# A one-core two-block transformer kernel: both memory attentions reordered by pairs of heads, cross-attention roots on GpSimd

## The reference

```python
def memory_attention(h, mem_n, wq, wk, wv, wo):          # 4 heads of 256
    q = (h @ wq).reshape(B, S, MEM_HEADS, MEM_HEAD_DIM)
    k, v = ...                                           # from mem_n
    s = jnp.einsum('bshd,bmhd->bhsm', q, k).astype(F32) * (MEM_HEAD_DIM ** -0.5)
    p = jax.nn.softmax(s, axis=-1).astype(v.dtype)
    return jnp.einsum('bhsm,bmhd->bshd', p, v).reshape(B, S, D) @ wo

def memory_cross_attention(h, mem_n, wq, wkv, q_g, k_g, wo):   # 4 heads of 128
    q = rms_norm_2((h @ wq).reshape(b, s, XA_HEADS, XA_HEAD_DIM), q_g)
    k, v = ...                                           # from mem_n, k normed
    logits = jnp.einsum("bshd,bmhd->bhsm", q.astype(jnp.float32), k.astype(jnp.float32)) * (XA_HEAD_DIM ** -0.5)
    p = jax.nn.softmax(logits, axis=-1)
    o = jnp.einsum("bhsm,bmhd->bshd", p, v.astype(jnp.float32)).astype(h.dtype)
    return o.reshape(b, s, XA_WIDTH) @ wo
```

## Time and profile before

| | us |
|---|---|
| three runs | 971.75, 972.66, 981.94 (median 972.66) |
| profiled execution, its own time | 978.42 |
| its span | 976.4 |
| TensorE busy in it | 910.1 (93%) |
| VectorE, ScalarE, GpSimd busy | 574.4, 406.6, 131.2 |
| mean granted TensorE clock | 0.958 |

### The profile page before, as it was taken

How to read it: one execution, slowest core, us unless ns; L and a number is a source line. 1 busy time by engine, 2 the same in 40 slices (tenths; PEclk the granted TensorE clock), 3 DMA queues, 4 the chain that set the end, 5 groups by cost and what they waited for, 6 DMA issues and landing times.

```text
span 976.4 us, 13578 instructions
## 1 busy us (share of the span) xinstructions
PE 910.1 (93%) x5642; PEld 789.4 (81%) x5642; DVE 574.4 (59%) x830; ACT 406.6 (42%) x554; POOL 131.2 (13%) x174
## 2 busy tenths in 40 slices
PE   6988998998999999999899888999998889999998
PEld 5986985686778999999687886677577679999997
DVE  4349456345359867775668983743454648555552
ACT  4348242334336445443546444312233426444440
POOL 0150000100010000000169860340000000000000
PEclk9997998999999999999998999799999799999999
DMA  8971444052236655654145231100163228656531
GB/s 289 288 231 48 179 166 147 27 195 92 80 136 231 209 186 171 210 174 130 44 134 171 88 130 44 44 1 4 40 215 114 60 76 290 195 181 202 178 130 44
DMA packets 92344, 136.01 MB, mean 139 GB/s; under 512 B 4435, under 2 KB 76763, under 8 KB 92028
## 3 DMA queue, kind: packets, MB, share of 16 engines
q1 hardware_dynamic: 90428, 129.90, 40.5%
q0 software_dynamic: 736, 2.63, 0.9%
q10 hardware_dynamic: 1120, 2.62, 0.8%
HBM read 133.56 MB, written 1.06 MB: 138 GB/s over the span
## 4 chain that ended last, share of the span: by engine, by line
PE 79%; DVE 11%; ACT 3%; issue 2%; POOL 2%; DMA 2%; SPq 0%; POOLq 0%; DVEq 0%; ACTq 0%
PE work L1973 30%; PE acc L1973 25%; PE work L1954 7%; PE work L2430 3%; DVE hT L1320 2%; DVE split_operands L1335 1%; PE acc L2464 1%; ACT act_junk L883 1%; PE work L2358 1%; PE work L2367 1%; DVE arena L1613 1%; PE work L1960 1%; DVE split_extra_slot L1335 1%; PE work L2125 1%; PE work L2227 1%
## 5 line engine op out<-in xcount | busy, mean ns | idle before, releaser
L1335 DVE TENSOR_TENSOR split_operands<-weight_ring,split_operands 128x2048 fp32r<-128x2048 f32 x72 | 165.8, 2305 | 89.6 <-ACT split_operands L903 89.1
L1973 PE MATMUL work<-split_operands 128*128 128x256 f32 x1680 | 208.1, 284 | 3.9 <-DVE split_operands L1335 3.9
L1973 PEld LDWEIGHTS work<-split_operands 128*128 128x128 f32 x1680 | 205.7, 193 | 6.2 <-issue 4.9
L1973 PE MATMUL acc<-split_operands 128*128 128x512 f32 x888 | 207.5, 390 | 1.8 <-DVE split_operands L1557 1.8
L1973 PEld LDWEIGHTS acc<-split_operands 128*128 128x128 f32 x888 | 165.1, 188 | 35.5 <-DVE split_operands L1557 2.0
L903 ACT ACTIVATE split_operands<-weight_ring 128x2048 fp32r<-128x2048 f32 x72 | 137.3, 1909 | 107.0 <-PE acc L1973 49.3
L1973 PE MATMUL work<-split_operands,split_extra_slot 128*128 128x256 f32 x1152 | 145.5, 287 | 4.5 <-DVE split_extra_slot L1335 4.5
L1973 PEld LDWEIGHTS work<-split_operands,split_extra_slot 128*128 128x128 f32 x1152 | 142.8, 195 | 6.7 <-issue 5.8
L890 ACT ACTIVATE arena<-work 128x512 f32<-128x512 f32 (+1 forms) x70 | 39.0, 560 | 167.6 <-PE work L1973 82.6
L1335 DVE TENSOR_TENSOR split_extra_slot<-weight_ring,split_extra_slot 128x2048 fp32r<-128x2048 f32 x34 | 78.4, 2307 | 41.1 <-ACT split_extra_slot L903 40.8
L903 ACT ACTIVATE split_extra_slot<-weight_ring 128x2048 fp32r<-128x2048 f32 x34 | 64.9, 1909 | 47.7 <-PE work L1973 17.8
(11 more groups left out here) (295 smaller groups left out, 953.2 us busy)
## 6 DMA issues: line engine op xcount, KB each, us to landing
weight_ring<-in_mlp_w SPq DMA_DIRECT2D x32, 1024.0 KB, 5.5
weight_ring<-in_w_up SPq DMA_DIRECT2D x22, 1024.0 KB, 5.1
weight_ring<-in_w_in SPq DMA_DIRECT2D x20, 1024.0 KB, 5.9
weight_ring<-in_w_down SPq DMA_DIRECT2D x11, 1024.0 KB, 5.0
weight_ring<-in_w_out SPq DMA_DIRECT2D x8, 1024.0 KB, 4.9
weight_ring<-in_w_mk SPq DMA_DIRECT2D x4, 1024.0 KB, 5.9
weight_ring<-in_w_mv SPq DMA_DIRECT2D x4, 1024.0 KB, 6.1
weight_ring<-in_w_mq SPq DMA_DIRECT2D x4, 1024.0 KB, 5.4
```

Source lines behind the costliest of these rows:

```text
L1335: dve.tensor_tensor(slot[:, 1, :], weights(split_units[i], 2048), slot[:, 0, :], ALU.subtract).then_inc(low_ready, 1)
L1973: ins = pe.matmul(out, lhs(p), rhs(q), start=(start and n == 0), stop=(stop and n == 2))
```

## The change

Four heads are two pairs. Scores, softmax, transposes and values are now done pair by pair. In the first attention the scores of pair 0 come after three of four query products, and the fourth product stands between them and their transposes; the first unit of `wo` stands between the transposes of pair 1 and the values of pair 1. In the cross attention the second query product is cut in halves (one head each), the sums and scores of pair 0 stand between the halves; `xwo`'s first unit is issued in pieces, with the last tile of transposes and the values of pair 1 between them. The one-column sums go to `acc` banks, by pair. Sqrt and reciprocal become an add on VectorE and a power on GpSimd (`xq_roots`), and ScalarE does one small exponential earlier, so that its table is loaded there. ScalarE's and VectorE's programs are reordered to match, weight splits included.

```diff
     norm("mem")
-    tiles.extend(("mq", c) for c in range(4))
-    tiles.extend(("ms", t, hp) for t in range(TT) for hp in range(2))
-    tiles.extend(("mpT", t, hp) for t in range(TT) for hp in range(2))
-    tiles.extend(("mo", c) for c in range(4))
+    tiles.extend(("mq", c) for c in range(3))
+    tiles.extend(("ms", t, 0) for t in range(TT))
+    tiles.append(("mq", 3))
+    tiles.extend(("mpT", t, 0) for t in range(TT))
+    tiles.extend(("ms", t, 1) for t in range(TT))
+    tiles.extend(("mo", c) for c in range(2))
+    tiles.extend(("mpT", t, 1) for t in range(TT))
+    tiles.extend(("mo", c) for c in range(2, 4))
...
     norm("cross")
-    tiles.extend((("xq", 0), ("xq", 1), ("xq_sums",)))
-    tiles.extend(("xs", t, hp) for t in range(TT) for hp in range(2))
-    tiles.extend(("xpT", t, hp) for t in range(TT) for hp in range(2))
-    tiles.extend(("xo", c) for c in range(2))
+    tiles.extend((("xq", 0), ("xq_head", 2), ("xs", 0, 0), ("xs", 1, 0), ("xq", 1)))
+    tiles.extend((("xpT", 0, 0), ("xpT", 1, 0), ("xs", 0, 1), ("xs", 1, 1)))
+    tiles.extend((("xo", 0), ("xpT", 0, 1), ("xpT", 1, 1), ("xo", 1)))
...
     fills = []
-    for product in ("mv", "o", "out", "wo", "down", "xv", "out2", "xwo", "m2"):
-        fills += [(product, i) for i in range(2 if product in ("o", "xv") else 4)]
+    for product in ("mv", "o", "out", "wo", "down", "xv", "out2", "xq_sums", "xwo", "m2"):
+        fills += [(product, i) for i in range(2 if product in ("o", "xv", "xq_sums") else 4)]
...
-            for stage in ("cross", "mlp"):
-                for t in range(TT):
-                    rstd((stage, t), False)
+            for t in range(TT):
+                rstd(("cross", t), False)
+            for hp in range(2):
+                pool.wait_ge(*acc_drained(("xq_sums", hp)))
+                pool.tensor_tensor(xq_root[:, hp], xq_root[:, hp],
+                                   conc("neg_half")[:, 0:4].rearrange("p (t j) -> p t j", t=TT), ALU.pow).then_inc(xq_roots, 1)
+            for t in range(TT):
+                rstd(("mlp", t), False)
...
             high_rows("mem")
-            for c in range(4):
+            def drain_queries(c):
                 drain(("mq", c), qmT[:, 2 * c:2 * c + 2, :], halves(("mq", c)), scale=MEM_DIM ** -0.5).then_inc(reader(("mq", c)), 1)
-                if c < 2:
...
-            m = TT
+            for c in range(2):
+                drain_queries(c)
+                high_parts(upto(("mq", 3)) + c)
+            high_parts(upto(("wo", 1)))
+            drain_queries(2)
+            for hp in range(2):
+                if hp:
+                    high_parts(upto(("wo", 2)))
+                    drain_queries(3)
+                for t in range(TT):
+                    act.wait_ge(neg_max, TT + 2 * hp + t + 1)
...
-            high_parts(upto(("wo", 2)))
             for c in range(4):
                 high_mix("wo", c, halves(("mo", c)), full(("mo", c)))
...
             high_rows("cross")
+            act.activation(xsoft[:, 0, 1, 0, 0:1], conc("neg_half")[:, 0:1], ACT.Exp)
             high_parts(upto(("xwo", 0)))
-            drain(("xq_sums",), xq_root, bank(("xq_sums",))[:, 0:8].rearrange("p (t h) -> p t h", t=TT), ACT.Sqrt,
-                  bias=eps_col(P * EPS)).then_inc(reader(("xq_sums",)), 1)
...
+            def cross_queries(h, n, name, at):
+                src = bank(name)[:, at:at + SEQ * n].rearrange("p (c t) -> p c t", c=n)
...
+            def cross_exps(hp):
+                for t in range(TT):
+                    act.wait_ge(x_max, 2 * hp + t + 1)
...
+            cross_queries(0, 2, ("xq", 0), 0)
+            cross_queries(2, 1, ("xq_head", 2), 0)
+            cross_exps(0)
+            cross_queries(3, 1, ("xq", 1), 0)
+            cross_exps(1)
             high_parts(upto(("m1", 0)))
             for c in range(2):
                 high_mix("xwo", c, halves(("xo", c)), full(("xo", c)))
...
             low_parts(upto(("wo", 0)))
-            for t in range(TT):
-                for hp in range(2):
+            def memory_maxima(hp):
+                for t in range(TT):
                     dve.wait_ge(*full(("ms", t, hp)))
...
+            def memory_weights(hp):
+                for t in range(TT):
                     dve.wait_ge(*drained(("ms", t, hp)))
...
-            for t in range(TT):
-                for hp in range(2):
-                    name = ("mpT", t, hp)
-                    dve.wait_ge(*full(name))
...
+            def memory_turned(t, hp):
+                name = ("mpT", t, hp)
+                dve.wait_ge(*full(name))
...
+            def memory_lows(c):
+                low_mix("wo", c, bank(("mo", c))[:, :].rearrange("p (c t) -> p c t", c=2)).then_inc(reader(("mo", c)), 1)
+            memory_maxima(0)
+            memory_weights(0)
+            low_parts(upto(("wo", 1)))
+            for t in range(TT):
+                memory_turned(t, 0)
+            memory_maxima(1)
+            memory_weights(1)
+            memory_lows(0)
+            memory_turned(0, 1)
+            memory_lows(1)
+            memory_turned(1, 1)
             low_parts(upto(("wo", 2)))
-            for c in range(4):
-                low_mix("wo", c, bank(("mo", c))[:, :].rearrange("p (c t) -> p c t", c=2)).then_inc(reader(("mo", c)), 1)
+            for c in range(2, 4):
+                memory_lows(c)
...
             low_parts(upto(("xwo", 0)))
-            dve.wait_ge(*drained(("xq_sums",)))
-            link(dve.reciprocal(xq_root, xq_root))
-            for t in range(TT):
-                for hp in range(2):
+            def cross_means(hp):
+                dve.wait_ge(*acc_filled(("xq_sums", hp)))
+                dve.tensor_scalar(xq_root[:, hp], acc(("xq_sums", hp))[:, 0:4].rearrange("p (t j) -> p t j", t=TT),
+                                  P * EPS, None, ALU.add).then_inc(acc_read, 1)
...
-                for hp in range(2):
+                    dve.wait_ge(xq_roots, hp + 1)
+                    dve.tensor_tensor(high, high, xq_root[:, hp, t], ALU.mult).then_inc(x_max, 1)
+            def cross_weights(hp):
...
+            def cross_turned(t, hp):
+                name = ("xpT", t, hp)
+                dve.wait_ge(*full(name))
...
+            def cross_lows(c):
+                low_mix("xwo", c, bank(("xo", c))[:, :].rearrange("p (c t) -> p c t", c=2)).then_inc(reader(("xo", c)), 1)
+            cross_means(0)
+            cross_maxima(0)
+            cross_weights(0)
+            cross_means(1)
+            for t in range(TT):
+                cross_turned(t, 0)
+            cross_maxima(1)
+            cross_weights(1)
+            cross_lows(0)
+            for t in range(TT):
+                cross_turned(t, 1)
             low_parts(upto(("m1", 0)))
-            for c in range(2):
-                low_mix("xwo", c, bank(("xo", c))[:, :].rearrange("p (c t) -> p c t", c=2)).then_inc(reader(("xo", c)), 1)
+            cross_lows(1)
             low_parts(upto(("m1", 1)))
             add_product("xwo")
...
+            def split_chunk(name, unit, stage, c):
+                ps = open_tile(name)
+                w = split_weights(unit, KD, 256)
+                for k in range(KD):
+                    ins = split_matmul(ps[:, 0:SEQ], lambda p: w[:, p, k, P * c:P * c + P],
+                                       lambda p: act_s[stage][p][:, k, :], k == 0, k == KD - 1)
+                ins.then_inc(tile_full, 1)
...
+            def split_steps(unit, first, last, lhs, steps):
+                w = split_weights(unit, 2, D)
+                for kk, t, half in steps:
+                    ins = split_matmul(acc((unit[0], 2 * t + half))[:, :], lambda p: lhs(p, kk, t),
...
-            for c in range(1, 4):
+            for c in range(1, 3):
                 split_pair(("mq", c), "mem")
-            for c in range(4):
-                pe.wait_ge(*drained(("mk", c)))
-                pe.wait_ge(*drained(("mq", c)))
...
+            for c in range(2):
+                pe.wait_ge(*drained(("mk", c)))
+                pe.wait_ge(*drained(("mq", c)))
+            memory_scores(0)
+            split_pair(("mq", 3), "mem")
+            memory_probs(0)
+            for c in range(2, 4):
+                pe.wait_ge(*drained(("mk", c)))
+                pe.wait_ge(*drained(("mq", c)))
+            memory_scores(1)
+            pe.wait_ge(*acc_drained(("mv", 3)))
+            for t in range(TT):
+                pe.wait_ge(*drained(("mpT", t, 0)))
+            for c in range(2):
+                memory_mixed(c)
+            memory_probs(1)
+            open_product("wo")
+            pe.wait_ge(*low_there(("mix", "wo", 0)))
+            split_product_unit(("wo", 0), True, False, wo_rows(0))
+            for t in range(TT):
+                pe.wait_ge(*drained(("mpT", t, 1)))
+            for c in range(2, 4):
+                memory_mixed(c)
+            pe.wait_ge(*low_there(("mix", "wo", 1)))
+            split_product_unit(("wo", 1), False, False, wo_rows(1))
```

(57 more changed lines are left out.)

99 lines of the change are left out of this document (35 added, 64 removed).

## The result

| | before | changed |
|---|---|---|
| median of 20 executions each, us | 977.62 | 969.71 |
| lowest, highest | 967.87, 985.32 | 965.23, 980.47 |
| profiled execution, its span | 978.42, 976.4 | 973.95, 972.2 |
| mean granted clock in it | 0.958 | 0.956 |

What follows compares the result with a forecast made beforehand. TensorE waits around the two memory attentions were taken as the recoverable loss. From the three-run median, 972.66 less 6.7 (5.0 first attention, 1.7 second) gave 966 us, 8-in-10 range 959.5 to 972.

Steps and rivals of the forecast that it cites:

- at full clock the second attention ends 4.7 earlier: Cross attention: the new order, its hole before xwo included, ends 4.7 us earlier if the clock stays full.
- gain 2.1: Cross attention: 4.7 us less about 2.6 lost to the 1.2 GHz level in xwo leaves 2.1.
- the 1.7 taken for the median: Cross attention: gain lowered from 2.1 to 1.7 us, as the median execution may have fewer half-clock stretches to recover.
- forecast of 6.7: Whole kernel: 6.7 us faster than the median of 972.66, from both attentions together.
- the same: Whole kernel: no difference that can be told, within about 1% or 9.7 us; chance 0.71.
- 5.2: First attention: TensorE waits for nothing in the new order, gaining 5.2 us, 5.0 with hand-overs.
- rival (d): First attention: a bank or weights come late, losing 3 of 5 us, 969; shares the 0.22 chance of rival (b).
- a hole of 4.3: Cross attention: TensorE idles 4.7 us less one tile of transposes, 4.3, before xwo, behind ScalarE's weight split.
- The fall of the clock in the hole: Cross attention: the hole before xwo likely drops TensorE to 1.2 GHz for about 5 us, costing about 2.6.
- rival (b): Cross attention: gives nothing, so 967.7, or up to 969 if the first attention gives 3.7; chance 0.22.
- Rival (a): Cross attention: the clock holds through the hole, 5.0 + 4.7 and a possible microsecond elsewhere, 962.5; chance 0.2.
- Rival (c): Cross attention: the clock stays at 1.2 GHz to the end of xwo, 8.4 us later, total 976.1; chance 0.05.

Runs made afterwards that it cites:

- e1: Kernel before with only the first attention's edit, cross attention in the old order; 0.9985 of the time before (0.9949 to 1.0021), 1.5 us faster.
- e3: Changed kernel with ScalarE making the high part of cross values 0 ahead of the xwo 1 weight split; 0.9904 of the time before, 9.4 us faster.
- e2: Kernel before with only the cross attention's edits, GpSimd roots included, first attention as before; 1.0007 of the time before (0.998 to 1.0034).
- e5: The file of e1 run again, for more executions; 0.993 of the time before (0.9898 to 0.9962), 6.9 us faster.
- e6: Kernel before with only the cross attention's roots changed (VectorE add, GpSimd power, table loaded earlier); 1.0015 of the time before (0.9982 to 1.0048).
- e8: The kernel before, unedited, run again for a second trace; 458.05 us between the attentions and 47.94 in the cross attention.
- e9: The file of e2 with the edit of e3; 0.9951 of the time before (0.9919 to 0.9984), 4.8 us faster.
- e4: Changed kernel with five plain matmuls that nobody reads in the TensorE hole ahead of xwo; 0.9948 of the time before (0.9915 to 0.998).
- e11: The kernel of e3 run again, for its interval and a second trace; 0.9897 of the time before (0.9856 to 0.9939), 10.1 us faster.

## Why the prediction was right or wrong

**The step that failed** is the value of the cross attention, "at full clock the second attention ends 4.7 earlier", and with it the "gain 2.1" and the 1.7 taken for the median. The end of the new order at full clock was subtracted from the end of the old one at half clock. The prediction had itself worked out that the scores and values of the earlier trace rows lost 3.0 and 1.8 to the clock; taken off first, the old order's stretch comes to 46.5, and `e1` measured 46.27. The new order with its full hole at full clock is 44.8, from `e3`'s 43.31 and the 1.5 of hole that it took away, or 44.5, from 46.36 less the 1.8: **1.5 to 1.7 us, not 4.7**. The hole's clock fall of 1.8 takes that back.

The 2.1 and 1.7 are closer to what came than this step deserves. What the new order gained against the old one as it usually ran is 2.9 us by the traces, nearly all of it half-clock time of the old order, and the prediction had no term for the last norm, which it expected to start as before: the clock fell over it and took back 1.7. The 1.1 that is left, an estimate, is not told apart from 1.7 by `e2`'s interval, nor from nothing. That the forecast of 6.7 lies inside 2.8 to 7.8 is in part luck.

**The other step that failed** is the border for telling a change. The prediction took 1% for the least that can be told, and put 0.71 on "the same". With 20 executions each the interval is 0.26% to either side, and 0.54% came, clear of it: "no change" was the wrong reading for a step of 5 us that the working of the first attention had found without a gap.

**Right:** the first attention. With the start and the slow first product taken off, 1.2 us together, every piece of the chain ended within 0.3 us of its forecast place, there was no wait, and 5.3 us (78.49 to 73.17 at a clock of 1.00 in `e3`) stands where 5.2 was written. The times of `e1` and `e5` give 4.2 (1.8 to 6.6). Weights reached TensorE in time: ScalarE waited 0.6 for `wo` 1, and TensorE never for ScalarE, so rival (d) did not happen. In the cross attention the chain that sets `xwo`'s start was right engine by engine; a hole of 4.3 was forecast, and 3.4 came, 2.57 behind the transposes and 0.8 ahead of them.

**The fall of the clock in the hole** was called likely; it came in both traces with the full hole (the changed kernel, `e2`), for 3.4 us and not about 5. The row that spoke against it, 1.00 from 230.07 to 236.89, is what the old first attention usually shows: the same waits and transposes were at 1.00 in `e2`, `e6` and `e8` too, and only in `e9` did the clock fall there, so that the values behind them took 9.36. What the Trainium skill says of transposes, that they do not count as busy in the way other matmuls do ("TensorE: Matmul & The Clock Gate", Part 4), thus stays possible; no run here isolates it.

**The sum** was then hung on a median of three. 972.66 was 5 below the median of 20, so 966 was too low as a place, although the difference of 6.7 lies inside the interval. That the profiled execution was 5.8 slower than the median was read in part as half-clock time in the cross attention; it was an ordinary execution, 0.8 above the median of 20, and `e5` repeated its cross stretch of 51.32.

**The rivals.** The change cannot tell rival (b), "the second attention gives nothing", 5.0 faster and a chance of 0.22, from the forecast: 5.3 lies between, nearer to (b). Its reason held in one trace of the old order out of five. Rival (a) was built on the same wrong 4.7. Rival (c) did not happen: the half-clock stretch ended after 3.4 us.

**Open:** why the clock fell in the scores of the old order in four traces and held in `e1`; whether the roots on GpSimd are worth up to 1.8 us by themselves; and whether the fall over the last norm (186.43 and 187.91 for 184.7) is more frequent with the new order: it is in the traces of the changed kernel, `e2`, `e3`, `e4` and `e9`, not in `e11`; with the old order it is in `e6`, not in both of before, `e1` or `e5`.

## What to carry to other kernels

Before two orders are compared from a trace, bring both to the same clock, and price the clock by itself: in how many traces of each order does it fall, and where? One trace can't say that; here one execution of the old order took 46.27 and two took 51.32. Filling TensorE's waits by interleaving pairs pays in full when every cover has been checked against the queue ahead of it on the other engines; the one item left ahead of a short producer (1.9 us of weight split before a 0.6 us high part) cost 3.1 us of the cross stretch, 46.36 against 43.31, more than the pairs gained there at equal clock. And where executions of one kernel spread over 1.8%, count executions before saying what can't be told, and read stage lengths at equal clock, which repeat to 0.02 us (43.29 to 43.31 in three traces, 73.17 and 73.18 in four).

## What the runs showed of the hardware that was not expected

The power on GpSimd depends on the columns: 0.56 us for one, 1.02 for four, 1.65 for eight, all on 128 partitions. Eight one-column float32 matmuls in one row, 16 records, took 1.92 us at a granted clock of 1.00 in `e1`, and 2.19 to 2.50 in the four others with the old order, where the clock was at 1.00 ahead of them and fell within them (0.84 over them in `e8`, 0.73 in `e6`). In the changed kernel the two groups of eight records took 0.79 and 0.81 at 1.00, and the clock held over them in all eight traces with the new order. The same code ran at different clocks from execution to execution: the old cross attention was seen at 1.00, 0.96, 0.89 and 0.87, in 46.27, 47.94, 49.70 and twice 51.32 us; the 49.70 is the one with its roots changed.
